# High parts of the weight slots made by ScalarE instead of GpSimd in both in-projections of a two-block model, and one weight transfer issued earlier

## The reference, cut to what matters

```python
for l in range(DEPTH):                       # DEPTH = 2
    h = rmsnorm(x, attn_norm[l])
    (q, kc, vc, ksl, vsl, kwn, vwn, gts, gq, gk, gv, ga, gr, uv) = split_columns(h @ w_in[l])
    o_nsa = nsa_mixer(...)
    o_gla = gla_mixer(gq, gk, gv, ga, gr, ...)
    o_sg = spatial_gating(uv, ...)
    x = x + concatenate([o_nsa, o_gla, o_sg], -1) @ w_out[l]
    x = x + (silu(h2 @ w_gate[l]) * (h2 @ w_up[l])) @ w_down[l]     # h2 = rmsnorm(x, ffn_norm[l])
```

## Time and profile before

| | |
|---|---|
| median of three runs | 1908.72 us |
| span of the profiled execution, first to last instruction | 1905.0 us |
| TensorE busy | 1856.9 us, 97% |
| GpSimd busy | 1505.0 us, 79% |
| VectorE busy | 1128.8 us, 59% |
| ScalarE busy | 665.8 us, 35% |
| mean granted TensorE clock | 0.990 |

### The profile page before, as it was taken

The page is one execution under the profiler, slowest core; times in us unless marked ns, Lnnn a source line. Parts: engine busy times, 40 slices in busy tenths (PEclk is TensorE's granted clock), DMA queues, the critical chain, the costliest instruction groups (busy, mean ns, idle before and its releaser), DMA issues.

```text
span 1905.0 us, 28070 instructions
## 1 busy us (share of the span) xinstructions
PE 1856.9 (97%) x10354; PEld 1467.3 (77%) x10354; DVE 1128.8 (59%) x1645; ACT 665.8 (35%) x1154; POOL 1505.0 (79%) x1033
## 2 busy tenths in 40 slices
PE   8998999999999999998999999999999999999997
PEld 6776678888888877765888888888877777778885
DVE  5678875574366456888546514767846667650342
ACT  5256653110011132766421001113556665640112
POOL 8993249997888898721898878888799999689994
PEclk9999999999999999999999999999999999999999
DMA  5241013443344223300234333542223323223231
GB/s 198 80 155 45 23 45 109 132 135 98 99 133 131 87 82 101 122 24 12 78 100 143 122 100 103 148 120 83 80 84 89 101 83 95 82 68 109 89 95 49
DMA packets 68689, 182.53 MB, mean 96 GB/s; under 512 B 23888, under 2 KB 24144, under 8 KB 68432
## 3 DMA queue, kind: packets, MB, share of 16 engines
q1 hardware_dynamic: 60480, 154.48, 26.5%
q10 hardware_dynamic: 8080, 26.32, 4.3%
HBM read 178.67 MB, written 2.10 MB: 95 GB/s over the span
## 4 chain that ended last, share of the span: by engine, by line
PE 79%; DVE 7%; POOL 7%; issue 3%; ACT 2%; DMA 0%; SPq 0%; POOLq 0%; DVEq 0%; ACTq 0%
PE PS L451 24%; PE PS L454 23%; PE PS L455 23%; POOL w_lo L2326 3%; POOL w_hi L2319 2%; POOL w_hi L2321 2%; DVE work L1882 2%; PE PS L986 1%; PE PS L741 1%; DVE PS L1838 1%; PE PS L687 1%; PE PS L583 1%; PE PS L907 1%; PE PS L944 1%; PE PS L703 1%
## 5 line engine op out<-in xcount | busy, mean ns | idle before, releaser
L2326 POOL TENSOR_TENSOR w_lo<-raw,w_hi 128x256 fp32r<-128x256 f32 (+2 forms) x606 | 790.3, 1304 | 64.9 <-ACT w_hi L1385 16.8
L2319 POOL TENSOR_SCALAR w_hi<-raw 128x512 fp32r<-128x512 f32 x226 | 371.9, 1646 | 210.0 <-PE PS L451 194.2
L451 PE MATMUL PS<-a_hi,w_hi 128*128 128x512 f32 x1168 | 464.5, 398 | 4.6 <-POOL w_lo L2326 3.7
L454 PE MATMUL PS<-a_lo,w_hi 128*128 128x512 f32 x1168 | 456.0, 390 | 0.0
L455 PE MATMUL PS<-a_hi,w_lo 128*128 128x512 f32 x1168 | 456.0, 390 | 0.0
L2321 POOL TENSOR_TENSOR w_hi<-raw,const 128x1024 fp32r<-128x1024 f32 (+1 forms) x192 | 340.2, 1772 | 98.9 <-PE PS L451 93.2
L451 PEld LDWEIGHTS PS<-a_hi,w_hi 128*128 128x128 f32 x1168 | 219.7, 188 | 60.6 <-issue 7.2
L455 PEld LDWEIGHTS PS<-a_hi,w_lo 128*128 128x128 f32 x1168 | 219.8, 188 | 46.4
L454 PEld LDWEIGHTS PS<-a_lo,w_hi 128*128 128x128 f32 x1168 | 219.9, 188 | 44.0 <-issue 0.7
L451 PE MATMUL PS<-b_hi,w_hi 128*128 128x512 f32 x552 | 223.1, 404 | 3.4 <-ACT zs L1458 2.9
L454 PE MATMUL PS<-b_lo,w_hi 128*128 128x512 f32 x552 | 215.9, 391 | 0.0
(11 more groups left out here) (338 smaller groups left out, 2688.6 us busy)
## 6 DMA issues: line engine op xcount, KB each, us to landing
raw<-weights SPq DMA_DIRECT2D x278, 512.0 KB, 3.5
work<-mod_w ACTq DMA_DIRECT2D x24, 512.0 KB, 3.5
work<-cmp_w ACTq DMA_DIRECT2D x4, 1024.0 KB, 7.1
proj<-cmp_w ACTq DMA_DIRECT2D x4, 1024.0 KB, 5.6
bias<-rpb SPq DMA_DIRECT2D x256, 12.0 KB
rgw<-rgw ACTq DMA_DIRECT2D x8, 256.0 KB, 2.7
out<-xc SPq DMA_DIRECT2D x8, 256.0 KB, 2.6
const<-const SPq DMA_DIRECT2D x1, 1436.5 KB, 15.2
```

The source lines that it names most:

```text
L451: ins = nc.tensor.matmul(out, wh, hi, start=start, stop=False)
L454: nc.tensor.matmul(out, wh, lo, start=False, stop=False)
L2319: G.tensor_scalar(w_hi[:, r, k, :], raw[:, r, k, :], 1.0, None, ALU.mult).then_inc(pool_chain, 1)
L2326: ins = G.tensor_tensor(w_lo[:, r, k, :], raw[:, r, k, :], w_hi[:, r, k, :].bitcast(F32), ALU.subtract)
```

## The change

ScalarE makes the high parts of slots 2 to 13 of the first layer and 97 to 108 of the second (slots three to fourteen of each in-projection), and the second half of slot 1. GpSimd makes only their remainders and waits for `high_ok`. In the first layer slots 1 (half) and 2 are made between `a_hi` and the squares, slot 3 after the squares, and the others at the start of the step that stands two slots earlier, ahead of `crossed`. Slot 1's transfer is issued ahead of x's tile 6.

```diff
+HIGH_EARLY = (2, 3, 4, 5, 6, 7, 8, 9, 10, 11, 12, 13, 97, 98, 99, 100, 101, 102, 103, 104, 105, 106, 107, 108)
...
-    BY_ACT = [PLAN.index(("in2", 0)) + n for n in range(4, 11)]
+    BY_ACT = list(HIGH_EARLY) + [PLAN.index(("in2", 0)) + n for n in range(4, 11)]
...
+            def high_part(n, k=slice(0, KT)):
+                act.wait_ge(raw_in[n % RING], 16 * (n // RING + 1))
+                if n >= RING:
+                    act.wait_ge(slot_used, n - RING + 1)
+                A(w_hi[:, n % RING, k, :], raw[:, n % RING, k, :], ACT.Copy).then_inc(high_ok.sem, 1)
+                act.wait_ge(high_ok.sem, high_ok.raised())
...
                 if l == 0:
+                    high_part(1, slice(KT // 2, KT))
+                    high_part(2)
                     for k in range(KT):
                         A(work[:, k, :], x[:, k, :], ACT.Square).then_inc(squares.sem, 1)
                         act.wait_ge(squares.sem, squares.raised())
+                if l == 0:
+                    high_part(3)
                 inverse_rms((l, "ss"), D)
...
                 for name, late in STEPS:
+                    if name in T and PLAN.index(("in", l, name)) + 2 in HIGH_EARLY[2:]:
+                        high_part(PLAN.index(("in", l, name)) + 2)
                     if name in MIDWAY:
                         crossed(MIDWAY[name])
...
                     if n in BY_ACT:
                         pass
+                    elif n == 1 and h == 1:
+                        pool.wait_ge(high_ok.sem, high_ok.seen_by("pool"))
...
             for k in range(0, KT, 2):
+                if k == KT - 2:
+                    sp.dma_start(raw[:, 1, :, :], w_sl[1]).then_inc(raw_in[1], 16)
                 sp.dma_start(x[:, k, :], a_x[:, k, :]).then_inc(x_in[k], 16)
-            for r in range(1, RING):
+            for r in range(2, RING):
                 sp.dma_start(raw[:, r, :, :], w_sl[r]).then_inc(raw_in[r], 16)
```

More of the change, by code:

```diff
@@ L1376, in _ @@
                         act.wait_ge(h_hi.sem, h_hi.raised())
[L1381 to L1386, removed]
             act.wait_ge(gain_ok.sem, gain_ok.seen_by("act"))
@@ L1407, in _ @@
                 if k in (2, 6):
-                    high_part(BY_ACT[(2, 6).index(k)])
+                    high_part(BY_ACT[len(HIGH_EARLY) + (2, 6).index(k)])
             act.wait_ge(pad_ok.sem, pad_ok.seen_by("act"))
@@ L1424, in _ @@
                 if m in HIGH_AT:
-                    high_part(BY_ACT[2 + HIGH_AT.index(m)])
+                    high_part(BY_ACT[len(HIGH_EARLY) + 2 + HIGH_AT.index(m)])
             inverse_rms(("n1",), D)
@@ L2321, in split @@
                         G.tensor_tensor(w_hi[:, r, k, :], raw[:, r, k, :], ones[:, k, :], ALU.mult).then_inc(pool_chain, 1)
-                    if n not in BY_ACT:
+                    if n not in BY_ACT and (n, h) != (1, 1):
                         pool.wait_ge(pool_chain, counted())
```

## The result

The changed kernel takes 1914.75 us in the median of five runs (1913.18 to 1917.74), the kernel before 1908.72 us: ratio 1.0037 over all these runs, interval 1.0027 to 1.0048. It is slower by 6.0 us in the medians and by 7.2 in the means. The profiled execution took 1914.64 us with a span of 1912.7 us, 7.7 us above the span before.

A forecast was written before the change was run, and what follows sets the result against it. GpSimd was taken to bound only the first layer's in-projection, TensorE the rest. Terms -1.05 + 2.5 + 1.9 = 3.35 us slower, added to the median 1908.7, gave 1912.0 us, no change; range 1907.0 to 1915.6.

The forecast's parts named there:

- The start: First layer's first slots: 2.1 us gained at slot 2, 1.7 lost to the clock, 0.95 gained, 0.3 lost; 1.05 gained.
- VectorE's three additions: First layer, ahead of `stats`: predicted to take 4.6 us, bounds 3.9 and 5.5, with the sum ready at 25.3 us.
- Slots 4 and 5: First layer: their waits of 0.5 and 0.44 us for GpSimd were to go, 0.95 us gained.
- slot 6: First layer: its high part stands behind ScalarE's step LB; 0.3 us charged for a new wait, bounds 0 and 0.5.
- The charge of 1.7 us for the clock: First layer, after the 2.2 us wait at `stats`: TensorE's clock falls to 0.50, costing 1.7 us, bounds 0 and 1.7.
- The crossings: Two per layer: Copies ahead of `crossed` add 4.36 us, VectorE returns 1.9; 2.5 us lost, 1.5 first layer, 1.0 second.
- the 3.7 of stretch: Lengthening of four VectorE operations ahead of each crossing, beside GpSimd, 3.7 us in all; half, 1.9 us, was to go.
- Slot 97: Second layer: its high part waits behind the root's exponential on ScalarE; new TensorE wait, 1.9 us lost, no clock fall charged.
- L6 to CV1: First matmul of level L6 to the first on `kc`, both layers: the prediction had no term here.
- the step of q0: ScalarE step: its idle time was to cover the Copy, at no cost as long as that lasts 1.09 us.
- The first rival: Clock falls in the second layer too, at slot 97's 1.8 us wait: 1.7 us more, 1913.7 or 1915.6 us; chance 0.28.
- the third rival: VectorE's stretch ahead of the crossings goes altogether: 1.9 us less, 1910.1 us; chance 0.15.

The follow-up runs named there:

- e4_cross: Changed kernel, but ScalarE does the crossed copy before the high part in the steps of kwn, kc and q0; 1906.86 us, ratio 0.9994.
- e8_three: Changed kernel with crossed copy before high part, slots 97 and 98 split by GpSimd alone, squares before slot 2's high part; 1904.84 us, ratio 0.9983.
- e9_delay: Changed kernel, but GpSimd makes the two high parts of slots 14 and 109 twice, putting its work 3.1 us later; 1909.90 us in one run.
- e10_four: As e8_three, but also with the high parts of slots 6 and 101 ahead of ScalarE's step LB; 1904.57 us, ratio 0.9980.
- e12_q0: Changed kernel, but the crossed copy comes before the high part in the step of q0 alone; 1913.49 us in one run.
- e3_keep97: Changed kernel, but slots 97 and 98 are split by GpSimd alone, as before; 1913.03 us, ratio 1.0030.
- e1_first: Changed kernel, but only the first layer's high parts go to ScalarE, the second layer's in-projection as before; 1910.86 us, ratio 1.0021.
- e7_light_before: Kernel before, but GpSimd leaves out most of its work in slots 14 to 20 and 109 to 115; 1909.16 us in one run.

## Why the prediction was wrong

The prediction said no change, +3.3 us; measured were +6.0 us, above the 3.8 us that it could tell from none, though inside its range. Point by point, for the profiled execution:

- **The start, -1.05 us predicted.** Slot 2 began at 26.34 us for 26.3, in part by luck: VectorE's three additions took 5.06 us for 4.6, so `stats` came at 25.78 for 25.3, and slot 2 followed it after 0.56 us for 1.0. Slots 4 and 5 brought 0.72 us for 0.95 (slot 5 at 45.56 for 48.34 us, 2.78 in all), slot 6 cost 0.5 for 0.3. The charge of 1.7 us for the clock was not due in this execution; over the ten profiled ones in which TensorE waited 1.96 us or more at `stats` it was in six. With it away the start gained 2.3 us up to slot 6.
- **The crossings, +2.5 us predicted.** The mechanism held: at each crossing the wait changed by the Copy's 1.09 us and by what VectorE's four operations gained or lost, +1.28, +0.07, +0.42 and -0.04 us. In the first layer 1.93 us less the 0.5 of slot 6, thus 1.43 for 1.5. In the second layer 2.52 less 0.5 for slot 101 (which I had left out) and 1.6 for the clock, thus 0.4 for 1.0. VectorE's four operations ahead of the crossings took 2.18, 1.71, 2.21 and 1.70 us, 7.8 for 10.44; 2.6 us of the 3.7 of stretch went, where I had let half go. The reading that TensorE already waited at all of them was wrong for the first of the first layer (0.13 us). The clock behind the first of the second layer was not in the sum, since no idle time as short had cost it in the rows that I had read. VectorE ahead of the crossings of the changed kernel (columns as in rows 10):

```profile
62.00:64.28 2.28, 2.18 (x4) 1.00 0.26 31
78.38:80.20 1.82, 1.71 (x4) 1.00 0.32 61
715.57:717.90 2.33, 2.21 (x4) 1.00 0.22 56
733.61:735.42 1.81, 1.70 (x4) 1.00 0.75 269
```

- **Slot 97, +1.9 us predicted.** Measured 2.08, with a wait of 1.82. Here the clock held, as said, but it fell behind the same wait in three of seven profiled executions, so that was luck.
- **L6 to CV1: no term in the sum, 3.1 us measured (1.41 + 1.67).** This is the step that failed. The prediction wrote of the step of q0 that the chain shows no wait there, that "ScalarE's idle time covers the Copy, and the cost is nothing"; at that crossing this held. But it let GpSimd's and VectorE's meeting count ahead of the four crossings alone, and there as a gain. With fewer operations per slot GpSimd comes to slot 14 earlier against VectorE's chain, and stretches its operations at other moments, in a stretch where TensorE stands close behind VectorE. The runs show it from three sides: it vanishes when GpSimd's work is taken out, when that work alone is moved, and when the Copy of slot 13 is moved. Taken off the whole time, as an estimate, they leave 2.9 us by the medians and 4.1 by the means, about the 3.8 us that could be told from no change.

Of the 4.35 us by which the profiled execution exceeds the sum, 3.08 are this step. The start (1.43 us less than its terms up to L0) and the second layer's crossings (1.52 us more) cancel, and that is luck: a fall of the clock that was charged in the one did not come, and one that was not charged came in the other. The first layer's crossings and slot 97 add 0.13 and 0.18 us, and 0.87 us lie behind CV1, where no term and no edit stands.

The first rival had the right sign for a wrong place: the clock fell in the second layer in the profiled execution, but at the crossing, not at slot 97. Of VectorE's stretch ahead of the crossings 2.6 of 3.7 us went, between the half of the forecast and the whole of the third rival; the difference weighs less than the term that was missing.

What stays open is which order of the two engines' operations makes the 1.3 us. Slot 14, or 109 in the second layer, at -0.75 to -0.47 and at +0.21 us from L6 loses it; at +0.64 and +1.72 (the two layers of the kernel before) and at +2.2 to +2.5 (`e4_cross`, `e8_three`, `e9_delay`, `e10_four`, `e12_q0`) it does not; nothing between +0.21 and +0.64 was tried. This start is a mark for where GpSimd's later operations fall, not itself the cause: in `e9_delay` the added operations begin 0.75 us ahead of L6, and nothing is lost.

## What to carry to other kernels

When an engine is relieved, look for every later stretch in which its operations lengthen those of an engine that has no slack, and give it a term of its own, loss or gain, even if nothing is edited there. When work is given to an engine in order, put it behind what others wait for: the same Copies behind the crossed copy instead of ahead of it turned 6 us lost into no difference. And keep the waits that a change makes apart from the clock falls that may follow them: a difference of one fall (1.7 us) between two executions is no sign of either version.

## What the runs showed of the hardware

TensorE's clock did not follow the length of the wait alone. Behind waits of 1.40 to 1.44 us at the first crossing the granted clock fell to 0.50 in 8 of 14 profiled cases (2 of 7 in the first layer, 6 of 7 in the second); behind the 1.82 us of slot 97 in 3 of 7; at `stats` it held after 2.31 us (`e3_keep97`) and fell after 2.08 in two runs (`e1_first`, `e4_cross`) while it held after 2.08 in the changed kernel; at slot 1 it fell after 1.99 us in the kernel before and held after 2.00 in `e7_light_before`, whose start is the same. The line of the table by stretch where it fell in `e4_cross`:

```profile
28.00:30.00 2.00, 2.00 (x6) 1.56 (x5) 0.00 (x0) 1.97 (x3) 0.00 (x0) 0.51 0.73 174
```

The prediction had drawn a border between 1.64 and 1.99 us from one case on each side; there is none in these runs. The case on the keeping side was a weak one: TensorE worked for only 2 us after that restart (1892.09 to 1894.08). What decides was not tried here. By the granted clock that each execution lists (span times one minus clock, averaged) the lower level cost 18.9 us in the 24 runs of the kernel before beside `e1_first`, and 21.0 us in the five of the changed kernel, so about 2 us of the slowdown are of this kind. The step of the listed clock, 0.001, is 1.9 us, which makes that rough.
